# RWKV stage of a two-block model: four more places for context rows in the third weight slot, and weight groups placed by a table

## The reference

```python
def peer_block(hb, w_q, sub_keys, u_tab, v_tab):
    ...
    expert = jnp.take_along_axis(cand_i, pos, axis=-1)
    g = jax.nn.softmax(top_s, axis=-1)
    u = u_tab[expert]
    act = jax.nn.gelu(jnp.einsum('nhkd,nd->nhk', u, hb).astype(jnp.float32))
    w = (g * act).astype(hb.dtype)
    return jnp.einsum('nhk,nhkd->nd', w, v_tab[expert])
```

## Time and profile before

| | |
|---|---|
| median of three runs | 3375.44 us (3370.27 to 3380.55) |
| the profiled execution | 3365.98 us, span 3364.1 us |
| first rwkv stage | about 363 to 551 us of the span |
| second rwkv stage | about 1003 to 1200 us of the span |
| PE, DVE, ACT, POOL busy | 2677, 2248, 586, 1211 us |
| mean rate of the DMA engines | 306 GB/s |

### The profile page before, as it was taken

One profiled execution on the slowest core, in us unless ns is written; L12 is line 12 of the kernel. 1 busy time (PEld: TensorE's weight loads), 2 busy tenths in 40 slices (PEclk: granted clock), 3 DMA queues, 4 the chain that ended last, 5 costly groups with the idle time before them and its releaser, 6 DMA issues.

```text
span 3364.1 us, 30927 instructions
## 1 busy us (share of the span) xinstructions
PE 2677.2 (80%) x10160; PEld 1779.6 (53%) x10160; DVE 2247.5 (67%) x5413; ACT 586.3 (17%) x1601; POOL 1211.3 (36%) x1028
## 2 busy tenths in 40 slices
PE   6898676899685869998887877777789977777776
PEld 2787555688574747886575332322247833323222
DVE  0538876788768576774958985655555499856555
ACT  1311201200011021001311111111124111111111
POOL 0002443345644424651323444444300044444442
PEclk8998776999897678998999999999989989999999
DMA  9337785789977657995657999999930379999997
GB/s 394 113 133 257 274 293 202 242 312 343 392 292 276 220 196 253 409 409 195 202 183 296 402 420 420 420 420 420 410 122 31 138 323 419 420 420 420 420 418 307
DMA packets 209376, 1029.23 MB, mean 306 GB/s; under 512 B 23392, under 2 KB 24928, under 8 KB 142784
## 3 DMA queue, kind: packets, MB, share of 16 engines
q0 software_dynamic: 147456, 805.37, 61.1%
q1 hardware_dynamic: 60480, 215.77, 17.1%
q10 hardware_dynamic: 1280, 6.11, 0.5%
HBM read 1021.98 MB, written 5.18 MB: 305 GB/s over the span
## 4 chain that ended last, share of the span: by engine, by line
PE 39%; DMA 30%; DVE 22%; issue 5%; ACT 2%; POOL 1%; SPq 1%; DVEq 0%; ACTq 0%; another core or an unknown queue 0%; POOLq 0%
DMA w_ring<-in_peer_uv,expert 16%; PE ps L1187 9%; PE ps L2251 4%; PE ps L1940 4%; DMA ctx_ring<-in_peer_uv,expert 4%; DMA own<-in_peer_uv,expert 4%; PE ps L1109 4%; PE ps L443 4%; PE ps L1648 3%; PE ps L1199 2%; DVE ctx_ring L1338 2%; DMA ctx_ring<-in_peer_u,ctx_expert 2%; DVE sum L1335 2%; DVE w_ring L2128 2%; DMA w_ring<-in_weights 2%
## 5 line engine op out<-in xcount | busy, mean ns | idle before, releaser
L2251 PE MATMUL ps<-w_ring,diag 128*128 128x512 f32 x1224 | 586.9, 620 | 177.4 <-ACT diag L2210 177.4
L2128 DVE SCALAR_TENSOR_TENSOR w_ring<-w_ring,htok 128x1024 f32<-128x1024 f32 x306 | 374.4, 1224 | 216.5 <-DMA w_ring<-in_peer_uv,expert 214.6
L2251 PEld LDWEIGHTS ps<-w_ring,diag 128*128 128x128 f32 x1224 | 228.7, 196 | 527.3 <-ACT diag L2210 286.6
L2098 POOL DMA_INDIRECT w_ring<-in_peer_uv,expert x306 | 337.5, 1103 | 447.7 <-PE ps L2251 396.7
L1318 POOL DMA_INDIRECT ctx_ring<-in_peer_u,ctx_expert x192 | 247.5, 1289 | 579.9 <-DVE ctx_ring L1338 299.1
L1187 PE MATMUL ps<-mix,w_ring 128*128 128x256 f32 x1408 | 309.3, 383 | 7.4 <-DVE mix L388 7.4
L1187 PEld LDWEIGHTS ps<-mix,w_ring 128*128 128x128 f32 x1408 | 270.8, 193 | 45.9 <-issue 8.2
L2210 ACT ACTIVATE diag<-consts_sb,w 128x128 f32<-128x128 f32 x512 | 177.6, 394 | 604.0 <-DVE w L2145 600.0
L1318 POOL DMA_INDIRECT ctx_ring<-in_peer_v,ctx_expert x148 | 184.0, 1243 | 235.4 <-DVE sum L1335 159.9
L2251 PE MATMUL ps<-ctx_ring,diag 128*128 128x512 f32 x416 | 212.0, 637 | 67.7 <-ACT diag L2210 67.7
L1338 DVE SCALAR_TENSOR_TENSOR ctx_ring<-ctx_ring,h_now 128x1024 f32<-128x1024 f32 x192 | 228.3, 1223 | 54.1 <-DMA ctx_ring<-in_peer_u,ctx_expert 46.2
(11 more groups left out here) (402 smaller groups left out, 4553.9 us busy)
## 6 DMA issues: line engine op xcount, KB each, us to landing
w_ring<-in_weights SPq DMA_DIRECT2D x392, 512.0 KB, 8.0
w_ring<-in_peer_uv,expert POOLq DMA_INDIRECT x306, 15.9
ctx_ring<-in_peer_u,ctx_expert POOLq DMA_INDIRECT x192, 5.6
ctx_ring<-in_peer_v,ctx_expert POOLq DMA_INDIRECT x148, 8.8
consts_sb<-in_consts ACTq DMA_DIRECT2D x1, 1867.0 KB, 9.8
ctx_more<-in_peer_v,ctx_expert POOLq DMA_INDIRECT x108, 10.8
ctx_ring<-in_peer_uv,expert POOLq DMA_INDIRECT x104, 15.9
cT_first<-in_ctx_by_feature ACTq DMA_DIRECT2D x1, 1024.0 KB, 15.8
```

Of the source, the lines that this page charges most:

```text
L2098: pool.indirect_dma_start(out=entry(e), out_offset=None, in_=table, in_offset=bass.IndirectOffsetOnAxis(ap=m.expert[:, blk, k:k + 1], axis ...
L2128: v.scalar_tensor_tensor(out=u, in0=u, scalar=1.0, in1=m.htok[:, blk, :], op0=ALU.mult, op1=ALU.mult, accum_out=b.dots[:, e:e + 1]).then_i ...
L2251: ins = pe.matmul(m.ps[:, 2 * blk + half, :], b.diag[:, e % DIAGS, :], entry(e)[:, D + half * 512:D + (half + 1) * 512], start=(k == 0), s ...
```

## The change

In rwkv, four more places for context rows are opened in the third weight slot (`LENT_SLOT` = 2, 4 x 1024 floats), so that eight are in use there. The phases are numbered anew: even ones use `ctx_more`, the odd ones (rwkv) the lent slot. A lent place opens when in_projection has joined; `PHASE_STAGES` lists the stage for each phase.

To keep the slot free, the groups from MOD 0 to UKV may not go there. `WeightRing` works the slots out beforehand: each group gets the slot whose last user is the oldest among those allowed, and `previous` names the group it waits for. SP's two calls load one group less ahead: in_projection up to MOD 1, rwkv up to UKV; OUT 0 follows in latent_heads. By the table MOD 0 follows IN 3 in its slot, MOD 1 follows IN 4, and MOD n+2 follows MOD n (before: MOD 0 followed IN 2, and MOD n+3 followed MOD n).

```diff
 WSLOTS = 3
+LENT_SLOT = 2
+PLACES = CTX_RING + 2 * CTX_MORE
...
+    def __init__(self, mem, images, sizes, kept_free):
+        last = [-1] * WSLOTS
+        self.slot_of, self.previous = [], []
+        for g in range(len(sizes)):
+            j = min((j for j in range(WSLOTS) if j != LENT_SLOT or g not in kept_free), key=lambda j: last[j])
+            self.slot_of.append(j)
+            self.previous.append(last[j])
+            last[j] = g
...
-            if done and g - WSLOTS >= g0:
-                eng.wait_ge(*done(g - WSLOTS - g0))
+            if done and self.previous[g] >= g0:
+                eng.wait_ge(*done(self.previous[g] - g0))
...
-            ring.load_to(sp, g0 + G_MOD + WSLOTS, g0 + G_IN, lambda n: (s.prod_done, last_tile[n]))
+            ring.load_to(sp, g0 + G_MOD + WSLOTS - 1, g0 + G_IN, lambda n: (s.prod_done, last_tile[n]))
...
-                ring.load_to(sp, g0 + G_MOD + WSLOTS + n + 1, g0 + G_MOD, lambda k: (s.mod_done, k + 1))
+                ring.load_to(sp, g0 + G_MOD + WSLOTS + n, g0 + G_MOD, lambda k: (s.mod_done, k + 1))
...
-LAYER_STAGES = 6
+PHASE_STAGES = (0, 1, 2, 7, 8)
...
-        if l == DEPTH or name == "rwkv":
+        if l == DEPTH:
             return -1
-        return l if name == "in_projection" else l + 1
+        return 2 * l if name == "in_projection" else 2 * l + 1 if name == "rwkv" else 2 * l + 2
...
-            narrow, more = list(range(CTX_RING)), list(range(CTX_RING, CTX_RING + CTX_MORE))
+            narrow, at = list(range(CTX_RING)), CTX_RING + CTX_MORE * (now % 2)
+            more = list(range(at, at + CTX_MORE))
...
-        return m.ctx_ring[:, j, :] if j < CTX_RING else m.ctx_more[:, j - CTX_RING, :]
+        if j < CTX_RING:
+            return m.ctx_ring[:, j, :]
+        j -= CTX_RING
+        return m.ctx_more[:, j, :] if j < CTX_MORE else m.w[:, LENT_SLOT, D * (j - CTX_MORE):D * (j - CTX_MORE + 1)]
...
-                pool.wait_ge(m.joined, JOINING * (first_stage + LAYER_STAGES * (self.opened[r] - 1) + 2 if self.opened[r]
-                                                  else first_stage))
+                pool.wait_ge(m.joined, JOINING * (first_stage + PHASE_STAGES[self.opened[r]]))
...
-        done = {(g_query + n) % WSLOTS: n + 1 for n in range(NG_PQ)}
+        done = {ring.slot_of[g_query + n]: n + 1 for n in range(NG_PQ)}
```

More of the change, by code:

```diff
@@ L201, in slot @@
     def slot(self, g):
-        return self.mem.w[:, g % WSLOTS, :]
+        return self.mem.w[:, self.slot_of[g], :]
     def pieces(self, g):
@@ L215, in load_to @@
                 eng.dma_start(self.slot(g)[:, c:min(c + PIECE, n)], image[:, c:min(c + PIECE, n)]
-                              ).then_inc(self.mem.w_landed[g % WSLOTS], 16)
+                              ).then_inc(self.mem.w_landed[self.slot_of[g]], 16)
         self.started = max(self.started, min(g1, len(self.sizes)))
     def landed(self, eng, g):
-        eng.wait_ge(self.mem.w_landed[g % WSLOTS], 16 * sum(self.pieces(n) for n in range(g % WSLOTS, g + 1, WSLOTS)))
+        eng.wait_ge(self.mem.w_landed[self.slot_of[g]],
+                    16 * sum(self.pieces(n) for n in range(g + 1) if self.slot_of[n] == self.slot_of[g]))
 def view(kt, n, off=0):
@@ L1274, in wide @@
     def wide(l, name):
[L1276 removed]
+        if l == DEPTH:
             return -1
[L1278 removed]
+        return 2 * l if name == "in_projection" else 2 * l + 1 if name == "rwkv" else 2 * l + 2
     def place_rows(self, wide):
         count = len(wide)
[L1284 removed]
+        user, phase = [-1] * PLACES, [-1] * PLACES
         self.slots, self.after, self.opened, self.turn = [], [], [], []
[L1286 removed]
+        uses = [0] * PLACES
         for r, now in enumerate(wide):
             left = next((n for n in range(2 * CTX_MORE) if r + n + 1 >= count or wide[r + n + 1] != now), 2 * CTX_MORE)
[L1289 removed]
+            narrow, at = list(range(CTX_RING)), CTX_RING + CTX_MORE * (now % 2)
+            more = list(range(at, at + CTX_MORE))
             first = next(n for n in range(count) if wide[n] == now)
@@ L1473, in build @@
         m.ctx_ring = sb("ctx_ring", [CTX_RING, D])
-        m.ctx_row_in = [nc.alloc_semaphore(f"ctx_row_in{j}") for j in range(CTX_RING + CTX_MORE)]
+        m.ctx_row_in = [nc.alloc_semaphore(f"ctx_row_in{j}") for j in range(PLACES)]
         m.ctx_used = nc.alloc_semaphore("ctx_used")
@@ L1483, in build @@
         m.ctx_expert, m.ctx_weight = sb("ctx_expert", [TT, SLOTS], U32), sb("ctx_weight", [TT, SLOTS])
-        ring = WeightRing(m, d.weights, d.sizes)
+        ring = WeightRing(m, d.weights, d.sizes, {FIRST_AT + l * G_FIRST_END + g for l in range(DEPTH) for g in range(G_MOD, G_OUT)})
         m.block = ctx.enter_context(nc.Block())
@@ L2022, with __init__ @@
 class Entries:
-    def __init__(self, m, i, g_query):
+    def __init__(self, m, i, ring, g_query):
         self.m, self.i = m, i
         spare = [[k * 2 * D // WSLOT, ((k + 1) * 2 * D - 1) // WSLOT] for k in range(ENTRIES - OWN - LENT - 1)]
-        done = {(g_query + n) % WSLOTS: n + 1 for n in range(NG_PQ)}
+        done = {ring.slot_of[g_query + n]: n + 1 for n in range(NG_PQ)}
         self.queries = {OWN + LENT + k: max(done[slot] for slot in slots) for k, slots in enumerate(spare)}
@@ L2307, in second_block @@
                         nc.sbuf_tensor(f"top_{i}", [P, PEER_HEADS, TOPK], F32) as top:
-                    entries = Entries(m, i, g)
+                    entries = Entries(m, i, ring, g)
                     peer_queries(nc, m, d, ring, g, i, m.xT, LATENTS, top)
```

1 line of the change is left out of this document (removed).

## The result

| | before | after |
|---|---|---|
| median of four runs each | 3376.32 us | 3344.49 us |
| lowest to highest | 3370.27 to 3380.55 | 3342.16 to 3346.78 |
| the profiled execution | 3365.98 (span 3364.1) | 3342.16 (span 3340.4) |
| pair products to chunks, first and second stage | 88.0 and 88.0 us | 75.0 and 75.2 us |
| chunks to the end of rwkv | 70.4 and 77.3 us | 73.9 and 72.8 us |

The ratio after to before is 0.9907, 95% interval 0.989 to 0.9925: 25 to 37 us less. The forecast was 21 us less, 3354, with a range of 3338 to 3368. Sign and range hold. The gain of the medians, 31.8 us, is about 10 us larger than the sum; the two profiled executions differ by 23.8 us. In the kernel after, the lines are L1351 for L1338, L780 for L770, L596 for L586, L607/L608 for L597/L598, L1531 for L1518, L224 for L215.

What follows compares the result with a forecast made beforehand. A chain of waits, DVE's for gathered rows with PE next, was taken to bound the rwkv stages. Gains of 2.9 + 3.0 + 6.5 + 8.9 - 0.2 = 21.1 us from 3375.4 gave 3354, range 3338 to 3368.

Steps and rivals of the forecast that it cites:

- the sum: Gain forecast over both rwkv stages: 2.9 + 3.0 + 6.5 + 8.9 - 0.2 = 21.1 us.
- The burst before level 0: Six rows before level 0 in rwkv: without row waits, 2.9 us go in the first stage, 3.0 in the second.
- The gaps of levels 1 to 5: Start of L770 less end of last L598 goes: 6.5 us first stage, 8.9 second, less 0.2 us.
- the transfers rival: Levels 2 to 4 of rwkv: transfers keep rows late; gain 9 to 16 us, say 3363; chance 0.22.
- The clock rival: Rwkv levels: without waits PE stays at 2.4 GHz, up to 14 us more; gain 29 to 36; chance 0.09.
- its own mechanism: In both rwkv stages, rows arriving in time for DVE give a gain of 16 to 27 us; chance 0.56.
- The weights: Modulation groups around rwkv are loaded one level later, with unchanged DMAs and bytes; costed at nothing.
- The cover: Time to spare for rwkv's later weight loads: 7.5 us, from 19.8 us available and a longest landing of 12.3.
- the late weights: Levels 3 to 5, both rwkv stages: PE held once landings pass 19.8 us; 3383 at twice 12.3; chance 0.04.
- After the levels nothing: After the levels DVE waits for no row in either rwkv stage, so no gain there.
- The table: Turned slots of later groups move one 1 MB gather earlier in the expert stages; costed at nothing, 5.6 us in range.
- What would show it: Rwkv signs: DVE's row waits under 5 us, L770 within 0.1 us of last L598, levels about 13.3 us.

Runs made afterwards that it cites:

- experiment 4: Changed kernel loading only the first of four DMAs of modulation groups 3, 4 and 5 in both layers; 3337.72 us, ratio 0.9895.
- experiment 7: Changed kernel with two extra PE products filling the gap at the end of levels 1 to 4, and five rows per level; 3323.31 us, ratio 0.9846.
- experiment 1: Changed kernel with its new weight slots and later loads, but rwkv's rows in the old four places alone; 3377.64 us, ratio 1.0006 to before.
- experiment 11: Kernel before, four places and old slots, with five rows per level instead of six, the saved rows taken before rwkv's last products; 3354.33 us, ratio 0.9941.
- experiment 5: Changed kernel with two extra PE products in the gap at the end of levels 1 to 4; 3339.83 us, ratio 0.9893.
- experiment 9: Changed kernel with filled gaps in the levels, five rows per level and extra products in the chunks; 3302.58 us, ratio 0.9783.
- experiment 12: Changed kernel with filled gaps in the levels, extra products in the chunks and four rows per level instead of six; 3306.60 us, ratio 0.9797.
- experiment 8: Changed kernel with small extra PE products in the gaps of the four chunks; 3318.36 us, ratio 0.9831.
- experiment 6: Changed kernel with five rows per level instead of six, the saved rows taken before the wait for rwkv's last products; 3340.62 us, ratio 0.9899.

## Why the prediction was right, and where it was off

*The burst before level 0*: 2.9 and 3.0 us were forecast. From the first pair product to the first group of level 0 it was 402.21 - 392.66 = 9.55 us before and 395.19 - 389.58 = 5.61 after, in the second stage 9.47 and 6.47: 3.9 and 3.0 us. The mechanism is right. The first stage gave 1.0 us more, and there the clock had a part: its two groups of pair products took 2.05 and 1.95 us instead of 3.78 and 3.01.

*The gaps of levels 1 to 5*: 15.4 less 0.2 us forecast, 11.9 us measured (15.5 to 3.6). The second stage gave 8.8 of its 8.9; in the first, levels 3 and 4 kept 3.3 us. The argument by which every row of a burst is in time took landings of 5.6 and 7.8 us; the median landing in these levels went from 6.0 to 10.6 us and the longest from 9.5 to 14.3, at full transfers. This is the transfers rival, in two of ten levels. With less weight traffic the rows were in time but for 0.9 us (experiment 4). By the Trainium skill (DMA: Bandwidth & Descriptors, Issuing engines are not separate DMA queues) transfers of all issuing engines interleave on the same DMA engines. The trace agrees: rows and weights both landed later.

*The clock*, which the sum left as it was: the rest of the part. In the two profiles the parts shortened by 25.8 us together, of which 6.9 are the bursts and 11.9 the gaps; 7.0 us are left. PE's own time in the ten levels fell by just as much, 5.8 us in the first stage, where PEclk rose from 0.75 to 0.89, and 1.1 in the second. With the 1.0 us of the pair products that is 8 us for which the sum had nothing. The clock rival came half true: the group of 2.05 us appears in one level of the first stage and its mean over ten levels fell by 0.56 us, but it stayed near 3.8 in others behind the same gap of 2.83 us. The rival's own price of up to 1.1 us per group was also low, since it took 2.65 us for the best; at full clock it is 2.05. Levels of 13.3 us were forecast; they last 12.6 in the mean, from 11.6 to 14.7.

The Trainium skill (TensorE: Matmul & The Clock Gate, the oscillation in real kernels) advises to keep TensorE from waiting for data between bursts. That agrees with experiment 7, in which all gaps of 0.92 us stood ahead of full speed. It would not explain the chunks, which ran at 0.68 with no wait for a transfer. The same page of the Trainium skill has a second failure mode, frequent short idle times between groups of products. It tells it of other products than these, and the chunks resemble it.

*What was luck*: that the parts came within 5 us of the sum. The gaps gave 3.3 us less than forecast and the clock 8 us for which the sum had no term. The gain of the medians, 31.8 us, lies outside the 16 to 27 that the prediction gave its own mechanism and inside the 29 to 36 of the clock rival, though the profiles give the clock only 8 of them; the wide range took it in.

*The execution the sum was made against*: it was 9.5 us under the median of three runs and 10.3 under that of four, and the prediction subtracted its gain from the median as if that difference lay elsewhere. The profiled execution of after is 2.3 us under its own median, so 23.8 us between the profiles and 31.8 between the medians fit together, but which stretches hold the other 8 us isn't shown. Two runs speak to it and disagree. Against experiment 1 (an execution of 3381.9 us, 4.3 over its median, with later weights) the parts of after are 182.4 - 150.2 = 32.2 us shorter, about the gain of the medians; by that the levels of before were short in its profile. Against the profile of before itself, the parts of experiment 11 are 19.2 us shorter, and that is the gain of its medians too. Much of what made before's execution short lies outside the parts: from the end of the first rwkv to the second stage's pair products it took 481.8 us, and between 484.2 and 489.6 in the thirteen other profiles.

*The weights*: cost nothing, as forecast (experiment 1). The cover did not hold, though. MOD 4 was issued from 424.18 on, its longest landing was 14.7 us, and its product began at 441.29:

```profile
424.18 1.78 SPq L224 DMA_DIRECT2D w_ring<-in_weights  x4
```

```profile
441.29 1.90 PE L1531 MATMUL ps<-w_ring,silu 128*32 128x512 f32 x8
```

From the first issue to the product that is 17.1 us instead of 19.8, since levels were shorter. The landing of 14.7 us is that of the last of the four DMAs, issued at 425.5, so the group was there at 440.2, with 1.1 us of cover and not 7.5. The prediction also counted the landing from the first of the four issues; the last comes 1.3 us later. In experiment 5 levels of 10.8 us used the cover up. The mechanism of the late weights was the right one to name; the size of the cover was taken from the traffic of before.

*After the levels nothing*: right. The stretch from the chunks on became 3.5 us longer in the first stage and 4.5 shorter in the second, at a PEclk between 0.64 and 0.72, and its repetition scatters alike; no wait for rows stands there. *The table*: from the first to the last gather the expert stages last as before within 1 us. The stages between the two rwkv stages, feed_forward among them, took 484.6 us instead of 481.8; no other profile is as short there as that of before (see above).

*What would show it*: DVE's waits of under 5 us were 5.5; L780 right behind PE in ten levels was eight; levels of 13.3 us were 12.6.

## What to carry over

Forecast what the relief of an engine brings from the gap ahead of each step that two engines must reach, not from the sum of its waits. Give TensorE's clock a term of its own: here it was worth 8 us in the change and 11 in experiment 11, with nothing of it in the sums. Use more than one execution: the ten gaps summed to 15.5 us in one profile and to 24.9 in another with the same places and a like median. Then ask what the shorter loop asks of the transfers: about the same bytes in 15% less time brought the share from 0.8 to 0.92 and the rows' landing from 6.0 to 10.6 us. Where PE comes last, look at its clock loop by loop before anything else is cut, and lift two limits that may hide one another in one run.

## What was not expected of the hardware

- TensorE's clock in a loop with gaps is not given by the gap: behind the same 2.83 us idle the same 16 products took 2.05 to 3.79 us. With 1.98 us of idle products put in, and 0.92 us of gap left, they took 2.05 us 24 times out of 24 (experiments 7, 9 and 12).
- The stretch of small products with gaps of 0.5 to 1.7 us ran at a granted clock of 0.63 to 0.72 in the mean. From 490 to 510 in the first stage of after it was 0.50, the lower level, with PE busy for 16.2 of 20 us. A few more products in these gaps, whose results nobody reads, lifted the mean to 0.88 and shortened each stage by 12 to 13 us (experiment 8).
- Full DMA engines moved 408 to 410 GB/s here with rows of 4 KB and weights mixed. The average of the part, 342 GB/s, hides that levels 3 and 4 ran at this limit.
- Not settled: what decides, at gaps of 2.83 us, in which level the clock is up. In the second stage of the change and of experiments 4 and 6 the same order of group times comes back within 0.08 us (3.68, 2.66, 3.78, 3.41, 2.97), in the repetition of the change it does not (3.79, 2.05, 2.57, 3.78, 3.78). The second stage of experiment 8 shares its first four with the repetition, within 0.01 us.
